# Winograd block sums of the gate weights: the first sum goes into the block that no product uses, another becomes a difference

## The reference

```python
def swiglu(h, w_gate, w_up, w_down):      # h 256 x 2048, w_gate and w_up 2048 x 5632, w_down 5632 x 2048
    return (jax.nn.silu(h @ w_gate) * (h @ w_up)) @ w_down
...
        h = rms_norm(x, ffn_norm[layer])
        x = x + swiglu(h, ffn_w_gate[layer], ffn_w_up[layer], ffn_w_down[layer]).astype(x.dtype)
```

## Time and profile before

| | |
|---|---|
| median of three runs | 1937.71 us |
| the profiled execution | 1938.14 us, span 1936.4 us |
| PE | 1924.4 us busy, 99% |
| DVE | 1396.6 us, 72% |
| ACT | 925.2 us, 48% |
| DMA | 380.92 MB, 197 GB/s |
| chain that ended last | PE 90%, DVE 8%, ACT 1% |
| mean granted TensorE clock | 0.998 |

### The profile page before, as it was taken

How to read it: one execution, slowest core, us unless ns; L and a number is a source line. 1 busy time by engine, 2 the same in 40 slices (tenths; PEclk the granted TensorE clock), 3 DMA queues, 4 the chain that set the end, 5 groups by cost and what they waited for, 6 DMA issues and landing times.

```text
span 1936.4 us, 21975 instructions
## 1 busy us (share of the span) xinstructions
PE 1924.4 (99%) x9268; PEld 1611.4 (83%) x9268; DVE 1396.6 (72%) x1044; ACT 925.2 (48%) x723; POOL 23.7 (1%) x85
## 2 busy tenths in 40 slices
PE   9999999999999999999999999999999999999998
PEld 7889999988888888888888887788888888888886
DVE  6656788855757868878779556756877868968755
ACT  6444334436434545545445345633544544645443
POOL 1000000000000000000000030000000000000000
PEclk9999999999999999999999999999999999999999
DMA  9555444455555654747666655464575765746762
GB/s 307 178 177 165 153 152 152 149 178 164 183 196 190 244 196 174 276 139 251 242 207 227 223 183 167 137 209 152 205 273 175 254 203 194 260 133 238 260 210 94
DMA packets 214874, 380.92 MB, mean 197 GB/s; under 512 B 5937, under 2 KB 55170, under 8 KB 214530
## 3 DMA queue, kind: packets, MB, share of 16 engines
q1 hardware_dynamic: 214560, 379.10, 57.3%
q10 hardware_dynamic: 226, 0.55, 0.1%
HBM read 377.53 MB, written 2.10 MB: 196 GB/s over the span
## 4 chain that ended last, share of the span: by engine, by line
PE 90%; DVE 8%; ACT 1%; issue 0%; DMA 0%; SPq 0%; ACTq 0%
PE main L1595 39%; PE main L1601 19%; PE main L1537 8%; PE aux L1617 5%; PE main L1539 4%; DVE lo L990 4%; DVE raw L996 4%; PE aux L1621 3%; PE main L1617 2%; PE aux L1544 2%; PE main L1621 2%; PE aux L1706 1%; ACT hi L634 1%; PE main L1648 1%; PE main L1650 1%; PE main L1649 1%
## 5 line engine op out<-in xcount | busy, mean ns | idle before, releaser
L634 ACT CAST hi<-raw 128x2048 fp32r<-128x2048 f32 (+1 forms) x389 | 742.5, 1909 | 778.6 <-PE main L1601 492.9
L990 DVE TENSOR_TENSOR lo<-raw,hi 128x2048 fp32r<-128x2048 f32 x316 | 719.6, 2290 | 322.2 <-ACT hi L634 322.2
L1595 PE MATMUL main<-hi,act 128*128 128x512 f32 x1968 | 470.0, 391 | 0.0
L1595 PEld LDWEIGHTS main<-hi,act 128*128 128x128 f32 x1968 | 368.1, 188 | 77.5 <-issue 1.9
L1595 PE MATMUL main<-hi,mid 128*128 128x512 f32 x1616 | 385.6, 391 | 0.0
L1595 PEld LDWEIGHTS main<-hi,mid 128*128 128x128 f32 x1616 | 301.7, 188 | 63.0 <-DVE mid L1257 0.5
L1601 PE MATMUL main<-lo,act 128*128 128x512 f32 x984 | 243.1, 389 | 0.0
L1537 PE MATMUL main<-act,hi 128*128 128x512 f32 x640 | 229.1, 401 | 0.0
L981 DVE TENSOR_TENSOR lo<-raw,hi 128x2048 fp32r<-128x2048 f32 x71 | 162.6, 2290 | 80.0 <-ACT hi L634 80.0
L1601 PEld LDWEIGHTS main<-lo,act 128*128 128x128 f32 x984 | 184.7, 188 | 38.3
L1601 PE MATMUL main<-lo,mid 128*128 128x512 f32 x808 | 199.6, 389 | 0.0
(11 more groups left out here) (180 smaller groups left out, 1329.9 us busy)
## 6 DMA issues: line engine op xcount, KB each, us to landing
raw<-in_ffn_w_gate SPq DMA_DIRECT2D x104, 1024.0 KB, 5.3
raw<-in_ffn_w_up SPq DMA_DIRECT2D x88, 1024.0 KB, 6.4
raw<-in_ffn_w_down SPq DMA_DIRECT2D x88, 1024.0 KB, 5.0
raw<-in_ab_w_in SPq DMA_DIRECT2D x55, 1024.0 KB, 5.1
raw<-in_ab_w_out SPq DMA_DIRECT2D x16, 1024.0 KB, 5.0
raw<-in_pool_w SPq DMA_DIRECT2D x4, 1024.0 KB, 5.5
xn<-in_x SPq DMA_DIRECT2D x4, 512.0 KB, 8.3
raw<-in_ab_w_in SPq DMA_DIRECT2D x2, 512.0 KB, 6.5
```

The source lines that it names most:

```text
L634: return nc.scalar.copy(out_, in_)
L990: V.tensor_tensor(lo[:, split_at(t), :], src, hi[:, split_at(t), :].bitcast(F32), ALU.subtract).then_inc(lo_ready, 1)
L1595: mm(o2[:, h, :], lhs[:, k0 + n, c, h * P:(h + 1) * P], w_hi, start=(first and c == 0 and n == 0), stop=False)
```

## The change

The first sum, b11 + b12, is written over b12 instead of b11. b11 stays as it was loaded, so that this sum has to wait for nothing but the two loads, and VectorE makes it before it waits for `hi` of slot 0. The second sum adds b22 to it in the same place. The third, b12 + b22, is now the difference of (b11 + b12 + b22) and b11, written over b11; it is made behind `lo` of slot 2, ahead of the fourth. `SOURCE`, `SUM_FOR` and the order in which places come free follow.

VectorE's order before: lo0, sum, sum, lo1, sum, lo2, sum, lo3. After: sum, lo0, lo1, sum, lo2, sum, sum, lo3.

```diff
--- before.py
+++ after.py
@@ -166,7 +166,7 @@
     while s < SLOTS:
         if s in BLOCK_OF:
             out[s] = b11, b12, b22, b21 = [take() for _ in range(4)]
-            free += [(b22.at, s + 3), (b11.at, s + 4), (b12.at, s + 5), (b21.at, s + 6)]
+            free += [(b22.at, s + 3), (b12.at, s + 4), (b11.at, s + 5), (b21.at, s + 6)]
             s += BLOCK
         else:
             out[s] = [take()]
@@ -176,7 +176,7 @@
 
 
 PLACES = places()
-SOURCE = (0, 0, 2, 0, 1, 3)
+SOURCE = (0, 1, 2, 1, 0, 3)
 
 
 def split_at(t):
@@ -191,7 +191,7 @@
 
 
 assert S_FFN0 % RING == 0
-SUM_FOR = {1: 1, 3: 3, 4: 2, 5: 4}
+SUM_FOR = {1: 1, 3: 2, 4: 3, 5: 4}
 
 
 def block_index(s0):
@@ -983,33 +983,30 @@
 
             def prepare(t):
 
-                ve.wait_ge(hi_ready, t + 1)
                 s0, i = BLOCK_OF.get(t, (t, 0))
                 at = [p.at for p in PLACES[s0]]
-                src = raw[:, at[SOURCE[i]], :]
-                V.tensor_tensor(lo[:, split_at(t), :], src, hi[:, split_at(t), :].bitcast(F32), ALU.subtract
-                                ).then_inc(lo_ready, 1)
-                if t not in BLOCK_OF:
-                    return
-
-                def add(a, b):
-                    V.tensor_tensor(raw[:, at[a], :], raw[:, at[a], :], raw[:, at[b], :], ALU.add
-                                    ).then_inc(sum_made, 1)
+
+                def add(a, b, op=ALU.add):
+                    V.tensor_tensor(raw[:, at[a], :], raw[:, at[b], :], raw[:, at[a], :], op).then_inc(sum_made, 1)
 
                 def loaded(n):
                     ve.wait_ge(raw_loaded[at[n]], 16 * PLACES[s0][n].lap)
 
-                if i == 0:
+                if t in BLOCK_OF and i == 0:
+                    loaded(0)
                     loaded(1)
-                    add(0, 1)
+                    add(1, 0)
+                ve.wait_ge(hi_ready, t + 1)
+                V.tensor_tensor(lo[:, split_at(t), :], raw[:, at[SOURCE[i]], :], hi[:, split_at(t), :].bitcast(F32),
+                                ALU.subtract).then_inc(lo_ready, 1)
+                if t in BLOCK_OF and i == 1:
                     loaded(2)
                     add(1, 2)
-                if i == 1:
-                    add(0, 2)
-                if i == 2:
+                if t in BLOCK_OF and i == 2:
+                    ve.wait_ge(sum_made, BLOCK_SUMS * block_index(s0) + 2)
+                    add(0, 1, ALU.subtract)
                     loaded(3)
-                    ve.wait_ge(sum_made, BLOCK_SUMS * block_index(s0) + 3)
-                    add(3, 0)
+                    add(3, 1)
 
             def empty(out_, s, job, crosses):
```

## The result

The changed kernel takes 1970.36 us, median of 5 runs (1969.51 to 1971.95), against 1937.71 of the kernel before: ratio 1.0166, interval 1.0155 to 1.0177. That is 32.6 us slower. The forecast was 25.8 us slower, 1963.5, with a range that ended at 1969.0. The direction, the place and the length of the new waits came as forecast; the time is 6.9 us over the forecast and 1.4 us outside the range. What the forecast had left out is TensorE's clock, which fell for a short time behind some of the new waits.

What follows compares the result with a forecast made beforehand. TensorE, 99% busy, was taken to bound the kernel, waiting on VectorE's lo3 in each block. 8 x (1.03 + 2.20) = 25.8 us on 1938.14 gave 1963.9, less 0.43 for the median: 1963.5 us, range 1960 to 1969.

Steps and rivals of the forecast that it cites:

- What sets the end: VectorE's lo3, the `lo` part for slot 3, sets the end in all 16 blocks; TensorE's waits total 6.8 us.
- Case A: K range behind the down projection, 8 times: lo3 starts 1.03 us later and TensorE loses all of it.
- Case B: K range behind the up projection, 8 times: lo3 starts 2.20 us later, and TensorE already waits for it.
- Costed at nothing: Later hi4 and hi5 (cover 4 us, or 2), lo4, exchanged freed places and VectorE's load and sum waits add nothing.
- VectorE's step of 2.20: Consecutive VectorE sums and splits start 2.20 us apart, though each lasts 2.29; the difference is taken as 2.20 too.
- Rival (c), the clock: TensorE's granted clock falls behind the longer stall, in Case B: 8 x 1.7 = 14 us more, 1977; 6%.
- (a): VectorE packs the new order, lo3 comes earlier and the 16 stalls go, at most 6.8 us: 1931; 3%.
- (b): No change: unseen slack, such as TensorE making up a stall later: 1938; 2%.
- (d): Loads behind Case B come late, costing 0.5 to 1 us in each such block: 1968 to 1972; 5%.

## Why the prediction was right, and where it was not

- *What sets the end.* Right. lo3 of each block, 16 times; the runs moved it by five orders of the same instructions, and the time followed each time.
- *Case A, +1.03.* Right: 1.02 by the stall (0.51 to 1.53), lo3 within 0.01. The hoist's gain at hi1 and its loss in idle time are both in the rows, and the run without it prices the hoist at 1.04.
- *Case B, +2.20.* Right: 0.34 to 2.54. What was won ahead of lo2 went into the wait for hi2, 0.88 to 2.04 idle. The run with sum 3 ahead of lo2 took 2.02 of it back.
- *Costed at nothing.* Right in what it claimed: ScalarE's new waits at hi4 and hi5 reached no product (no wait of TensorE for a `hi` of a block), and the load for sum 1 in B, the 1.24 us wait, hid in the idle time. The cover in B was larger than I had put it: sum 4 ends at 652.91 and hi5 at about 654.84, product 5 would begin at 660.54 - 1.62 = 658.92 without the fall, so 4 us and not 2.
- *VectorE's step of 2.20.* Right. The rule that I had weighed against it, the Trainium skill's VectorE: DVE Perf Modes, "The DRAIN you can't avoid", would have had 2.29 from start to start. I had left out what the same section adds: a next operation that is not held starts earlier. The rows agree with that addition. The two sums after are 4.49 in one piece, 2.20 + 2.29. The measured time agrees with the sum by that rule, 1970, by accident: the stall lengths in this trace are those of the 2.20 steps.
- *Rival (c), the clock.* **This is the step that failed.** I priced it at 1.7 us a fall, about right (1.5 to 1.6), but took it as all or nothing, gave it 6% and put it at nothing in the sum, on the argument that a stretch fully busy around a stall of 2.4 us was unlike the start, which had been half idle. In the profiled execution it came behind 4 of the 8 stalls in B and added 6.5 us, nearly all of the 6.9 by which the time is over the forecast. Behind stalls of 2.5 us it fell in 16 of 32 (three executions: 4 and 5 of the 8 in the changed kernel, 7 of 16 without the hoist). The only row that I had of it was the earlier trace rows, from another kind of stretch and from one execution; that fall came in neither profiled execution of the changed kernel. The kernel before had no such stall over 0.51 in this stage. So little spoke for or against a fall behind 2.5 us, and with stalls as long as those which I forecast myself the range should have gone from 1963.5 to 1977. The Trainium skill, TensorE: Matmul & The Clock Gate, section "HAM oscillation — how this bites in real kernels", describes a fall after each wait between bursts, for waits of 3 to 5 us. The runs agree at 3.8 us, and at 2.8, below its waits, they show the same (16 of 16 together, in one execution); at 2.5 the fall came half the time.
- *Rivals (a), (b), (d).* None took place. VectorE could not pack the order, because lo1 in A waited 1.81 us for hi1, which waited for TensorE's slot, and lo2 in B 2.04 us for hi2, which stands behind the up projection's bank; nothing made up for a stall; the loads behind B added no wait.

## What to carry to other kernels

Before an operation is made independent of a wait, find the operation that the bounding engine waits for, and count what stands ahead of *that* in the queue after its last outside release. Work that moves ahead of a release wins behind it only what the release itself comes earlier by (1.0 us in A, nothing in B); work that moves behind the release costs its whole length, 2.20 us here. When a change makes stalls of TensorE of 2.5 us or more, as here, price a fall of its clock for each, beside the stall itself; between 1.8 and 2.5 us nothing was measured. Where such a stall cannot be avoided, matmuls of no use in the gap can pay for themselves: 64 of them won 7.3 us here.

## What the runs showed of the hardware that was not expected

In this stage, where TensorE is otherwise without a gap, the granted clock fell behind none of the stalls of 1.8 us or less (in the kernels with filled stalls, with sum 3 early and with sum 4 late on the changed one, 56 waits, and A's 16 waits of 1.53 in the two executions of the changed kernel), behind 16 of 32 of 2.5 to 2.6, and at 16 of 16 of 2.8 and 3.8. What decides at 2.5 us whether it falls stays open. The first matmuls behind a stall can still be fast, as in the block above, where the granted clock changes at 656.69, 1.5 us behind the end of the stall; but in the kernel without the hoist it changed at 922.70, 0.16 us before the end of one. A fall costs 1.5 to 1.6 us, as much as the stall in A.
